# Moving the page-table and beta/alpha weight loads to GpSimd's queue, and making the cache row numbers once a layer beside the projection

## What is computed

```python
for l in range(DEPTH):                                   # DEPTH = 2
    xp = xp + half_ffn(xp, norm_ffn1[l], w1_gate[l], w1_up[l], w1_down[l])
    xs = xs + half_ffn(xs, norm_ffn1[l], w1_gate[l], w1_up[l], w1_down[l])
    mix_p, new_p = mixing_prompt(rms_norm(xp, norm_mix[l]), lp)
    mix_s, new_s = mixing_sample(rms_norm(xs, norm_mix[l]), lp, state_conv[l], state_delta[l],
                                 cache_win_k[l], cache_win_v[l], cache_k[l], cache_v[l], page_table)
    xp = xp + mix_p @ w_out[l];  xs = xs + mix_s @ w_out[l]
    xp = xp + half_ffn(xp, norm_ffn2[l], ...);  xs = xs + half_ffn(xs, norm_ffn2[l], ...)
...
def mixing_sample(h, lp, conv_buf, s0, win_k, win_v, pool_k, pool_v, page_table):
    a_qkv, a_z, a_b, a_a, q_b, k_b, v_b, q_c, k_c, v_c = split_projection(h, lp['w_in'])
    ...
    k_past = pool_k[page_table].reshape(bsz, past, H_C, 2 * DC)
    v_past = pool_v[page_table].reshape(bsz, past, H_C, DV_C)
```

## Time and profile before

| | us |
|---|---|
| median of 3 runs | 3308.28 (3301.86 to 3313.04) |
| the profiled execution | 3307.32 |
| its span in the profile | 3305.6 |

### The profile page before, as it was taken

How to read it: one execution, slowest core, us unless ns; L and a number is a source line. 1 busy time by engine, 2 the same in 40 slices (tenths; PEclk the granted TensorE clock), 3 DMA queues, 4 the chain that set the end, 5 groups by cost and what they waited for, 6 DMA issues and landing times.

```text
span 3305.6 us, 45920 instructions
## 1 busy us (share of the span) xinstructions
PE 2995.1 (91%) x16542; PEld 2434.1 (74%) x16542; DVE 1525.8 (46%) x2818; ACT 666.2 (20%) x1261; POOL 172.0 (5%) x201
## 2 busy tenths in 40 slices
PE   4999999997788789999979999999878978899996
PEld 3888877877765468888768888788776655688885
DVE  4444445335554444445354453453455543544544
ACT  1111001223264211110011100122343541111000
POOL 2000000000032000000000000000002310000000
PEclk7999999998899889999989999999888988899998
DMA  6432122220068623222232312222104684233121
GB/s 150 116 83 81 57 84 60 67 80 0 29 193 239 182 77 89 76 75 59 71 104 76 88 49 83 69 68 63 55 0 137 204 231 121 64 82 83 52 80 62
DMA packets 365169, 301.07 MB, mean 91 GB/s; under 512 B 20946, under 2 KB 336556, under 8 KB 364850
## 3 DMA queue, kind: packets, MB, share of 16 engines
q1 hardware_dynamic: 340060, 213.88, 23.3%
q0 software_dynamic: 24960, 85.21, 8.2%
HBM read 287.20 MB, written 14.45 MB: 91 GB/s over the span
## 4 chain that ended last, share of the span: by engine, by line
PE 83%; DVE 6%; ACT 3%; DMA 2%; issue 2%; DVEq 1%; SPq 1%; ACTq 0%; POOL 0%; POOLq 0%
PE banks L673 30%; PE banks L729 17%; PE banks L785 13%; PE banks L696 5%; PE banks L1191 4%; PE banks L639 3%; PE banks L859 2%; PE banks L867 1%; PE banks L871 1%; DMA arena<-in_cache_win_v 1%; PE banks L1026 1%; PE banks L1090 1%; DVE normed_or_mixed L1606 1%; DMA arena<-in_cache_v,layer_cache_rows 1%; ACT weight_slots L1454 1%
## 5 line engine op out<-in xcount | busy, mean ns | idle before, releaser
L785 PE MATMUL banks<-normed_or_mixed,weight_slots 128*128 128x272 f32 x1792 | 418.3, 396 | 10.5 <-DVE normed_or_mixed L1606 10.5
L785 PEld LDWEIGHTS banks<-normed_or_mixed,weight_slots 128*128 128x128 f32 x1792 | 344.3, 192 | 82.8 <-DVE normed_or_mixed L1606 11.9
L673 PE MATMUL banks<-arena 128*128 128x272 f32 x1408 | 347.6, 402 | 15.4 <-DVE arena L1631 15.4
L673 PE MATMUL banks<-normed_or_mixed,arena 128*128 128x272 f32 x1408 | 337.1, 393 | 0.0
L673 PEld LDWEIGHTS banks<-arena 128*128 128x128 f32 x1408 | 274.6, 195 | 75.3 <-DVE arena L1631 17.7
L673 PEld LDWEIGHTS banks<-normed_or_mixed,arena 128*128 128x128 f32 x1408 | 268.1, 190 | 54.5
L1251 ACT ACTIVATE hidden_or_projected<-banks 128x1024 f32<-128x1024 f32 (+4 forms) x160 | 137.1, 864 | 226.9 <-PE banks L639 148.0
L729 PE MATMUL banks<-hidden_or_projected,keys_values_by_token 128*128 128x272 f32 x704 | 177.0, 393 | 0.0
L729 PE MATMUL banks<-hidden_or_projected,weight_slots 128*128 128x272 f32 x704 | 169.2, 393 | 0.0
L729 PE MATMUL banks<-arena,keys_values_by_token 128*128 128x272 f32 x704 | 169.2, 393 | 0.0
L639 PE MATMUL banks<-constants,hidden_or_projected 128*128 128x128 f32 (+2 forms) x880 | 133.3, 303 | 27.7 <-DMA hidden_or_projected<-in_x_sample 11.9
(11 more groups left out here) (371 smaller groups left out, 4348.7 us busy)
## 6 DMA issues: line engine op xcount, KB each, us to landing
weight_slots<-in_w_down SPq DMA_DIRECT2D x128, 256.0 KB
weight_slots<-in_w_in SPq DMA_DIRECT2D x28, 1024.0 KB
keys_values_by_token<-in_w_gate SPq DMA_DIRECT2D x48, 512.0 KB, 5.0
keys_values_by_token<-in_w_up SPq DMA_DIRECT2D x48, 512.0 KB, 5.2
weight_slots<-in_w_gate SPq DMA_DIRECT2D x40, 512.0 KB, 4.9
weight_slots<-in_w_up SPq DMA_DIRECT2D x40, 512.0 KB, 5.1
hidden_or_projected<-in_cache_win_k SPq DMA_DIRECT2D x112, 128.0 KB, 4.3
weight_slots<-in_w_down SPq DMA_DIRECT2D x64, 192.0 KB
```

The lines of the kernel that those rows point to most:

```text
L673: mm = pe.matmul(ps[:, bank, 0:HALF], weights[:, k, :], acts[:, k, :], start=first and k == 0, stop=k == 3, skip_group_check=True)
L785: mm = pe.matmul(half(bank + 2 * u, h), wslot[:, slot, at:at + 128], hT[:, k, h * HALF:(h + 1) * HALF], start=k == 0, stop=k == KD - 1)
```

## The change

The two beta/alpha loads and the twelve page loads are issued by GpSimd at the head of its list, under the semaphore `in_pages` (14 in all). `in_lam` counts 6 loads where it counted 8. VectorE makes no row numbers in the setup. In each layer, between the projection's norm and `project`, it waits for `in_pages`, copies the layer's beta/alpha weights, converts the page numbers into a scratch (the tile `bias_cn`, which is written later in the layer) and makes the layer's 64 row numbers; the layer's offset is a new constant `loff`. `layer_vecs` is counted there. The two copies at the layer's head and the tile `cache_rows` are gone.

```diff
@@ sync
-            for l in range(DEPTH):
-                ld(all_ba[:, l], A["w_in"][l, :, BA_COL:BC_COL].rearrange("(k p) n -> p k n", p=128), "in_lam")
-            for pg in range(4):
-                src = bass.AP(tensor=A["page_table"].tensor, offset=pg, ap=[[0, 32], [4, 32]])
-                sp.dma_start(page_of[32 * pg:32 * pg + 32, 0, :], src, allow_slow_non_contiguous=True)\
-                    .then_inc(s["in_pages"], 16)
-                for g in range(2):
-                    src = bass.AP(tensor=A["page_table"].tensor, offset=64 * g + 16 * pg, ap=[[0, 32], [1, 16]])
-                    sp.dma_start(page_of[32 * pg:32 * pg + 32, 1, 16 * g:16 * g + 16], src,
-                                 allow_slow_non_contiguous=True).then_inc(s["in_pages"], 16)
@@ gpsimd
+            for l in range(DEPTH):
+                st(all_ba[:, l], A["w_in"][l, :, BA_COL:BC_COL].rearrange("(k p) n -> p k n", p=128), "in_pages")
+            for pg in range(4):
+                src = bass.AP(tensor=A["page_table"].tensor, offset=pg, ap=[[0, 32], [4, 32]])
+                gp.dma_start(page_of[32 * pg:32 * pg + 32, 0, :], src, allow_slow_non_contiguous=True)\
+                    .then_inc(s["in_pages"], 16)
+                for g in range(2):
+                    src = bass.AP(tensor=A["page_table"].tensor, offset=64 * g + 16 * pg, ap=[[0, 32], [1, 16]])
+                    gp.dma_start(page_of[32 * pg:32 * pg + 32, 1, 16 * g:16 * g + 16], src,
+                                 allow_slow_non_contiguous=True).then_inc(s["in_pages"], 16)
             gp.wait_ge(s["setup_ev"], 11)
@@ scalar, and vector likewise
-            act.wait_ge(s["in_lam"], 16 * 8)
+            act.wait_ge(s["in_lam"], 16 * 6)
@@ vector, setup
-            dve.wait_ge(s["in_pages"], 16 * 12)
-            cp(row_f[:, :], page_of[:, :, :].rearrange("p a n -> p (a n)"))
             dve.drain()
-            dve.tensor_scalar(row_f[:, :], row_f[:, :], float(PAGE // 4), C("p32"), ALU.mult, ALU.add)
-            dve.drain()
-            for l in range(DEPTH):
-                dve.tensor_scalar(cache_rows[:, l, :], row_f[:, :], float(l * POOL_PAGES * PAGE // 4), None, ALU.add)
-            dve.drain()
@@ vector, layer
-                cp(lay_rows[:, :], cache_rows[:, ds(l, 1), :].rearrange("p l n -> p (l n)"))
...
-                cp(lay_ba[:, :, :], all_ba[:, ds(l, 1)].rearrange("p l k n -> p (l k) n"))
...
-                dve.tensor_tensor(sign, sign, C("m0"), ALU.add).then_inc(s["layer_vecs"], 1)
+                dve.tensor_tensor(sign, sign, C("m0"), ALU.add)
...
                 norm(l * 3 + 1, lay_norm[:, 8:16])
+                dve.wait_ge(s["in_pages"], 16 * 14)
+                alone(dve)
+                cp(lay_ba[:, :, :], all_ba[:, ds(l, 1)].rearrange("p l k n -> p (l k) n"))
+                cp(row_f, page_of[:, :, :].rearrange("p a n -> p (a n)"))
+                dve.drain()
+                dve.tensor_scalar(row_f, row_f, float(PAGE // 4), C("p32"), ALU.mult, ALU.add)
+                dve.drain()
+                dve.tensor_scalar(lay_rows[:, :], row_f, C("loff")[:, ds(l, 1)], None, ALU.add).then_inc(s["layer_vecs"], 1)
                 project(l)
```

More of the change, by code:

```diff
@@ L49, in columns @@
                     ("lm", 7 * 128), ("tri4", 32), ("neg4", 128), ("blk4", 32), ("bsel", 8), ("comb", 64),
-                    ("offc", 16), ("offb", 8), ("esum", 64), ("m0", 1), ("m1", 1), ("eps", 1), ("one", 1), ("lam0", 2), ("oml", 2), ("p32", 1)):
+                    ("offc", 16), ("offb", 8), ("esum", 64), ("m0", 1), ("m1", 1), ("eps", 1), ("one", 1), ("lam0", 2), ("oml", 2), ("p32", 1), ("loff", 2)):
         where[name] = (at, at + n)
@@ L99, in constant_arrays @@
     put("eps", np.full((128, 1), EPS))
+    put("loff", np.tile(np.arange(DEPTH) * float(POOL_PAGES * PAGE // 4), (128, 1)))
     put("one", np.ones((128, 1)))
@@ L168, in trunk @@
         page_of = sb("page_of_row", 2, 32, dt=I32)
-        cache_rows = sb("cache_rows", DEPTH, 64, dt=U32)
         lay_rows = sb("layer_cache_rows", 64, dt=U32)
@@ L228, in trunk @@
         lam_prod, r_end = carve(arena, r_end, 2, DEPTH * 32)
-        row_f, _ = carve(arena, 9600, 64)
+        row_f = bias_cn[:, :, :].rearrange("p g n -> p (g n)")
         y_rows, _ = carve(work, 0, 5, D)
@@ L1558, in _ @@
             dve.drain().then_inc(s["x_new"], 1)
-            dve.wait_ge(s["in_lam"], 16 * 8)
+            dve.wait_ge(s["in_lam"], 16 * 6)
             for i in range(2):
```

## The result

The changed kernel takes 3314.66 us (median of 19 runs, 3308.16 to 3322.56) against 3309.39 for the kernel before (19 runs, 3301.86 to 3313.71, and among them one slow one of 4077.19, which the ratio leaves out): ratio 1.0019 [1.0013, 1.0025], 4 to 8 us slower. The forecast was 7.1 us faster, 3301.2, with a range up to 3313. The sign was wrong, and the time lies 1.7 us above the range; it is within the 0.3% that the forecast gave 0.56. The profiled execution took 3312.02 us (3307.32 before), with a span of 3310.3.

The account below looks back on a forecast made before the run. TensorE is busy for 91% of the span, but in the setup gap the moved requests set the pace from 11.35 to 46.72 us. 13.76 + 1.3 + 0.8 - 8.8 = 7.1 us less: 3301.2 us, range 3293 to 3313.

Parts of the forecast that it names:

- Parts 1 to 3: The forecast's three gains, in the setup and at the layers' heads: 13.76, 1.3 and 0.8 us, together 15.9.
- part 4: Setup: the same packets on POOL's queue delay SP's packets ahead of `in_lam`; cost 8.8 us, bounds 0 and 21.0.
- Part 1: Setup: the page table leaves VectorE's path, so the layer's first copy moves from 46.72 to 32.96; gain 13.76 us.
- Part 2: Setup: `in_lam` no longer waits for the beta/alpha loads, released at 20.1 instead of 21.39; gain 1.3 us, bounds 0 and 1.97.
- Part 3: Layer heads: two copies fewer, 0.40 us a layer, gain 0.8; the work reappears beside the projection, covered, cost 0.
- Part 5: First gate weights: landing at about 38.5 us, before VectorE needs them at 42.1; covered by 3.6 us, cost 0.
- Part 6: VectorE's instruction stream: the issue gap at layer 1's head may shift either way; 0, bounds -4 to +5 us.
- high end of part 4: Setup, bucket engines: 272 page packets an engine at 72 ns, 19.6 us, and 1.4 of beta/alpha: 21.0 us.
- rival B: Bucket engines before `in_lam`: moved packets pass in blocks ahead of SP's, costing 21.0 us; 3313.4 us, chance 0.15.
- 64 page packets: Evidence for rival B: POOL's table store waited about 5 us, read as 64 page packets of 72 ns, one whole load's share.
- the smaller figures: Setup: lower costs of the moved packets: 3.6 us at the low end, about 2 in a rival of chance 0.32.
- usual start: POOL's queue: some 2 us from issue to first bytes, read from the last stretch, issue at 3291.78.

Follow-up runs that it names:

- e1_tail: The changed kernel with GpSimd's fourteen beta/alpha and page loads moved behind its bias-table transfers, ahead of its layer loop: 3294.46 us, 0.9959 of the kernel before.
- e7_one_tail: The changed kernel with one whole-table load replacing the twelve page loads, it and the two beta/alpha loads behind GpSimd's bias-table transfers: 3294.85 us, 0.9953 of the kernel before.
- e4_sp: The changed kernel with the fourteen loads back in their old place on SP's queue, only the later row numbers kept: 3308.26 us, 0.9994 of the kernel before.
- e3_act: The changed kernel with the fourteen loads issued on ScalarE's queue, at the head of its program, instead of GpSimd's: 3305.9 us, 0.9991 of the kernel before.
- e6_double: The changed kernel with each of the four single-number page loads issued twice, the second into an unread tile: 3332.99 us, 1.0067 of the kernel before.
- e5_one: The changed kernel with one load of the whole table in 128-number runs replacing the twelve page loads at GpSimd's head: 3298.31 us, 0.9959 of the kernel before.

## Why the prediction was wrong

**What held.** Parts 1 to 3 were about right as a sum for the setup. Without part 4's cost they put the layer's first copy at 32.96 - 1.3 = 31.7; with the packets out of the way it comes at 32.21 (e1_tail) and 31.98 (e7_one_tail). Their 15.9 us are 13.6 [8.3, 18.9] and 15.6 [11.3, 20.2] by the comparisons.

- Part 1 left out its condition. The 13.76 us are gained only because the page requests leave SP's queue as well; e4_sp gains them at 32.44 and gives them back to the gate weights by 48.08.
- Part 2 said 20.1 for `in_lam`; without POOL's packets it is 20.63 and 20.39. The gain is 0.8 to 1.0, not 1.3, in the bounds given.
- Part 3: from the layer's first copy to the weight arithmetic 1.72 us now (51.19 to 52.91) against 2.00 (46.72 to 48.72): 0.28 a layer, not 0.40. Beside the projection VectorE's waits are 110.5 us in 14, as good as the 110.9 before: the cover held.
- Part 5: no wait for gate weights in the changed kernel, as forecast, though with everything some 16 us later than the forecast had it (first gate issue at 40.33, not near 24). Its landing of "about 38.5" does not come out of its terms (23.8 + 4.6 + 9.2 = 37.6), which changes nothing. The cover is gone where SP's page issues stand ahead (e4_sp).
- Part 6: at layer 1 the two gaps are 3.13 + 4.05 against 3.23 + 5.21: 1.3 us gained, in the bounds.

**The step that failed** is in part 4, word for word "For the share that stands ahead I let each SP packet wait for one page packet", and with it the 8.8 us. It took a packet to be one page number of 72 ns, as on SP's queue. On POOL's queue the packet that SP's packets wait for is an engine's whole share of a load, 64 numbers and 3.6 to 4.3 us. With turns of about one packet each, that is not 103 x 72 ns but nearly all of POOL's time: 19.0 us at the layer's first copy in place of 8.8. It also moved the place: x, whose landing was to be 3 to 4 us later, was 19.5 later.

The high end of part 4, 21.0, was thus nearly the truth, and rival B, chance 0.15, was the case: "the moved packets pass in blocks", 3313.4 against 3314.66 measured. That its price fits so well is partly luck: it took 72 ns a number from the pace of SP's queue, and POOL's blocks happen to take 57 to 67. So was its evidence: the table store that stood for "64 page packets" stood beside SP's single numbers, where there are no blocks. What spoke for the smaller figures, 8.1 ns of recorded time a packet and engines nine tenths idle, came from SP's queue as well, where each number is a packet by itself. None of these rows could price the same load on POOL's queue.

Why that store stood is open. POOL waited for it 11.29 us in the kernel before and 11.80 in e4_sp, both with the pages on SP's queue, and 5.11 in e1_tail, without them; so single numbers on SP's queue seem to hold another queue too, though on ScalarE's queue they cost x only 0.9 us (e3_act). The "usual start" of 2 us beside it was misread: POOL issued at 3291.78 and bytes moved from 3292.9, 1.1 us later. At the head of its list, with the first issue at 1.43, POOL's queue moved nothing before 6 us.

The Trainium skill, DMA: Bandwidth & Descriptors, section Queues, rings and completion order, has an engine take the queues by turns and change only at the end of a packet, which may hold up to 64 descriptors. The traces are near it: 382 packets of SP's to 291 of POOL's over 12 to 37 us of e6_double, and 64 numbers in each of POOL's blocks. The section Issuing engines are not separate DMA queues has another issuer save only the issuer's time; by that alone the cost would be the 21.0 of the high end, near what came. But the runs show the limit of that rule: the loads are 6,624 packets from SP or ScalarE and 448 from POOL, and from ScalarE, as far as they met x and the broadcasts, they cost these 0.9 and 1.5 us (e3_act), so which queue they stand on does matter.

Open is why a number takes 57 to 67 ns on POOL's queue, and why the blocks are longer in the changed kernel than in e6_double: no run changed the size of a number.

## What to carry to other kernels

Before a load moves to another engine's queue, ask what a packet is on that queue: read the packet counts by queue, not the bytes or the issue times. Here many single numbers on GpSimd's queue went out in long packets, and whatever was in flight on SP's queue paid for them turn by turn; bring such a table as a few long runs and let an idle engine pick out the numbers, or place the load where the bound engine already has its operands. And a wait that is taken off one engine's path is gained only if nothing else waits behind the same requests.

## What the runs showed of the hardware that was not expected

- The same load has another number of packets on another queue: 64 a load and engine from SP or ScalarE, one from POOL (6,624 against 448 for the fourteen loads, signals counted).
- Small runs are far cheaper than single numbers on POOL's queue. In e5_one POOL's packets up to 8.0 us are those of the two beta/alpha loads, each of 1,024 runs of 32 bytes; they took 2.2% of 0 to 8 us, 0.18 us an engine: about 0.1 us for the 64 runs of one load, where 64 single numbers take 3.6 to 4.3.
- To issue such loads took long on the hardware queues: ScalarE was at it until 31.56 us (e3_act), SP until 34.31, POOL was done with the same fourteen at 10.53.
